# A two-layer hybrid network on one core: 512 columns per matmul in the dense products, activation buffers 64 bytes beyond a multiple of 128, norm totals from a rounded part and its rest

## What is computed

```python
def rmsnorm(x, g):
    y = x32 * lax.rsqrt(jnp.mean(x32 * x32, axis=-1, keepdims=True) + NORM_EPS)
    return (y * g).astype(x.dtype)
def conformer_conv(h, ...):            # layer 1 in place of the recurrence
    u = h @ w_in + b_in                # "cin"
    u = u[..., :D] * jax.nn.sigmoid(u[..., D:])
    u = causal_dwconv(u, dw) + dw_b    # 31 taps
    u = jax.nn.silu(layernorm(u, ln_g, ln_b))
    return u @ w_out + b_out           # "cout"
def conv_ffn(h, w_in, dw, w_out):      # "up" 1024 -> 5632, "down" 2816 -> 1024
    u = causal_dwconv(h @ w_in, dw)
    gate, val = u[..., :D_FF], u[..., D_FF:]
    return (jax.nn.silu(gate) * val) @ w_out
x = x + out; x = x + attention(rmsnorm(x, ..)); x = x + conv_ffn(rmsnorm(x, ..), ..)
```

## Time and profile before

| | |
|---|---|
| median of 3 runs | 2604.6 us (2602.82 to 2608.18) |
| profiled execution, on the device | 2604.33 us |
| its span, first to last instruction | 2602.5 us |
| instructions | 62231 |
| TensorE busy | 2506.9 us, 96% of the span, 25266 matmuls |
| VectorE, ScalarE, GpSimd busy | 1340.9, 1122.6, 995.2 us |
| mean granted TensorE clock | 0.986 |
| moved over DMA | 219.43 MB, mean 84 GB/s |

### The profile page before, as it was taken

One profiled execution on the slowest core, in us unless ns is written; L12 is line 12 of the kernel. 1 busy time (PEld: TensorE's weight loads), 2 busy tenths in 40 slices (PEclk: granted clock), 3 DMA queues, 4 the chain that ended last, 5 costly groups with the idle time before them and its releaser, 6 DMA issues.

```text
span 2602.5 us, 62231 instructions
## 1 busy us (share of the span) xinstructions
PE 2506.9 (96%) x25266; PEld 2367.6 (91%) x25266; DVE 1340.9 (52%) x2035; ACT 1122.6 (43%) x1652; POOL 995.2 (38%) x488
## 2 busy tenths in 40 slices
PE   6999898999999999998999999999999999999998
PEld 6888796997999999977989999999998769999998
DVE  7657554613477741798533677612143344455521
ACT  7834455454444433334534344433244444444422
POOL 3324220461444444325322444444443104444442
PEclk8899999999999999999999999999999999999999
DMA  4221001251232233323212322233222103322232
GB/s 147 74 65 59 2 1 63 82 194 38 94 97 95 91 102 100 130 65 105 90 65 65 97 94 91 92 111 114 88 93 69 49 1 97 97 89 97 96 99 74
DMA packets 62180, 219.43 MB, mean 84 GB/s; under 512 B 6752, under 2 KB 9184, under 8 KB 61408
## 3 DMA queue, kind: packets, MB, share of 16 engines
q1 hardware_dynamic: 58880, 207.76, 24.4%
q10 hardware_dynamic: 3168, 9.75, 1.1%
HBM read 213.29 MB, written 4.19 MB: 84 GB/s over the span
## 4 chain that ended last, share of the span: by engine, by line
PE 83%; DVE 8%; issue 6%; ACT 2%; POOL 1%; DMA 0%; DVEq 0%; POOLq 0%; ACTq 0%
PE psum L571 70%; DVE psum L2698 5%; PE psum L713 3%; PE psum L721 2%; PE psum L1072 1%; PE psum L1021 1%; PE psum L1251 1%; POOL wl L520 1%; PE psum L1290 1%; DVE psum L2267 1%; PE psum L1253 0%; ACT wh L1382 0%; PE psum L683 0%; PE psum L1278 0%; PE psum L690 0%
## 5 line engine op out<-in xcount | busy, mean ns | idle before, releaser
L520 POOL TENSOR_TENSOR wl<-raw,wh 128x1024 fp32r<-128x1024 f32 x388 | 949.0, 2455 | 1464.0 <-ACT wh L1382 1463.6
L571 PE MATMUL psum<-acth,wh 128*128 128x256 f32 x3792 | 763.8, 283 | 20.6 <-DVE actl L2789 8.2
L571 PE MATMUL psum<-actl,wh 128*128 128x256 f32 x3792 | 753.9, 281 | 0.0
L571 PE MATMUL psum<-acth,wl 128*128 128x256 f32 x3792 | 753.3, 280 | 0.0
L1382 ACT ACTIVATE wh<-raw 128x1024 fp32r<-128x1024 f32 x388 | 407.1, 1056 | 625.1 <-PE psum L571 601.4
L571 PEld LDWEIGHTS psum<-acth,wh 128*128 128x128 f32 x3792 | 582.7, 189 | 38.1 <-issue 30.2
L571 PEld LDWEIGHTS psum<-acth,wl 128*128 128x128 f32 x3792 | 581.7, 189 | 0.0
L571 PEld LDWEIGHTS psum<-actl,wh 128*128 128x128 f32 x3792 | 581.5, 189 | 0.0
L2628 DVE TENSOR_TENSOR cu<-psum,rstd 128x512 f32<-128x512 f32 x132 | 91.1, 690 | 236.9 <-PE psum L571 219.6
L571 PE MATMUL psum<-hidh,wh 128*128 128x256 f32 x1056 | 210.0, 277 | 0.0
L571 PE MATMUL psum<-hidh,wl 128*128 128x256 f32 x1056 | 209.5, 277 | 0.0
(11 more groups left out here) (442 smaller groups left out, 4048.3 us busy)
## 6 DMA issues: line engine op xcount, KB each, us to landing
raw<-in_weights SPq DMA_DIRECT2D x388, 512.0 KB, 3.3
xt<-in_x SPq DMA_DIRECT2D x4, 512.0 KB, 5.4
xt<-in_x ACTq DMA_DIRECT2D x1, 2048.0 KB, 9.3
out_x<-xt SPq DMA_DIRECT2D x6, 256.0 KB, 2.3
mem<-in_mem ACTq DMA_DIRECT2D x1, 1024.0 KB, 11.0
memn<-memh ACTq DMA_DIRECT2D x1, 1024.0 KB, 7.0
memn<-meml ACTq DMA_DIRECT2D x1, 1024.0 KB, 10.0
memh<-memn ACTq DMA_DIRECT2D x1, 1024.0 KB, 4.7
```

The source lines that it names most:

```text
L520: pool.tensor_tensor(wl[:, s, :], raw[:, s, :], wh[:, s, :].bitcast(F32), ALU.subtract).then_inc(split_done, 1)
L571: ins = pe.matmul(out[:, n:n + HALF], w, m[:, n:n + HALF], start=first and n == 0, stop=last and n + HALF >= out.shape[1])
```

## The change

- `product` issues one matmul for all columns of a term: 512, or 256 over the memory tokens.
- The cursor is moved on by 32 bytes ahead of `acth`, which lies at 67648 then, `actl` at 84032; small buffers change places behind them so that `zone` stays where it was. The ones become a buffer of their own of type fp32r, set by VectorE; `eps` shares a buffer with the parameters.
- The norm totals in front of xattn, ffn, conv, in2 and for the memory: ScalarE rounds the sum of squares into `sums[0]` (`sum_high`), VectorE subtracts for the rest `sums[1]` (`sum_low`), and TensorE sums both over the partitions in fp32r, four matmuls of 256 columns. The first norm, the layer norm and the last norm keep the fp32 total (`exact_total`).
- These totals come behind tile 1, where they came behind tile 0 (in o behind tile 2).

```diff
...
         n = KT if split else 0
-        self.take(stage, sq=KT, rstd=1, split=n, val=n)
+        self.take(stage, sq=KT, rstd=1, split=n, val=n, sums=n // KT)
...
         xt = place("xt", [P, KT, T + 1])
+        cursor[0] += 32
         act_at = cursor[0]
+        assert act_at % P == 64
         acth = place("acth", [P, KT, T], F32R)
         actl = place("actl", [P, KT, T], F32R)
-        par = place("par", [P, NPAR])
-        common = place("common", [P, 3 * P])
+        par = place("par", [P, NPAR + 6])
+        eps = par[:, NPAR:NPAR + 6]
+        sq_at = cursor[0]
+        sq = place("sq", [P, 2, T])
+        sums = at("sums", [P, 2, T], F32R, sq_at)
         omu = place("omu", [P, 7 * KT])
-        eps = place("eps", [P, 6])
+        common = place("common", [P, 2 * P])
+        ones_r = place("ones", [P, P], F32R)
         tmp_at = cursor[0]
         tmp = place("tmp", [P, 2, T])
-        sq_at = cursor[0]
-        sq = place("sq", [P, 2, T])
         rstd_at = cursor[0]
...
         zone = cursor[0]
-        ident, ones, blk64 = (common[:, j * P:(j + 1) * P] for j in range(3))
+        ident, blk64 = (common[:, j * P:(j + 1) * P] for j in range(2))
+        ones = ones_r[:, :].bitcast(F32)
+        assert zone % 512 == 192 and sq_at % 64 == 32
         b_eps, b_ln, b_gn, b_rn, b_q, b_eps2 = (eps[:, j:j + 1] for j in range(6))
...
-        room = [[act_at, act_at + 32768], [yx_at, yx_at + 16384], [xt_at, xt_at + 16384], [tmp_at, tmp_at + 10240]]
+        room = [[act_at, act_at + 32768], [yx_at, yx_at + 16384], [xt_at, xt_at + 16384], [tmp_at, tmp_at + 6144], [sq_at, sq_at + 4096]]
...
             sp.dma_start(common[:, :], dram["c_common"]).then_inc(common_in, 16)
-            sp.dma_start(par[:, :], dram["par"]).then_inc(par_in, 16)
+            sp.dma_start(par[:, 0:NPAR], dram["par"]).then_inc(par_in, 16)
             with sp.Fori(0, UNITS // SLOTS) as i:
...
                 for w, m, first, last in ((w_h, hi, start, False), (w_h, lo, False, False), (w_l, hi, False, stop)):
-                    for n in range(0, out.shape[1], HALF):
-                        ins = pe.matmul(out[:, n:n + HALF], w, m[:, n:n + HALF], start=first and n == 0,
-                                        stop=last and n + HALF >= out.shape[1])
+                    ins = pe.matmul(out, w, m, start=first, stop=last)
                 return ins
...
-            def norm_total(stage, n=T):
+            def exact_total(stage):
                 pe.wait_ge(sq_used, plan(stage, "sq") + KT + SC)
-                pe.matmul(bank[4][:, 0:n], ones, rstd[:, 0:n], start=True, stop=True).then_inc(sum_mm, 1)
+                pe.matmul(bank[4][:, :], ones, rstd[:, :], start=True, stop=True).then_inc(sum_mm, 1)
+
+            def norm_total(stage, n=T, to=4):
+
+                pe.wait_ge(sum_lo, plan(stage, "sums") + 1)
+                for j in range(2):
+                    for c in range(0, n, HALF):
+                        ins = pe.matmul(bank[to][:, c:c + HALF], ones_r[:, :], sums[:, j, c:c + HALF], start=j == 0 and c == 0,
+                                        stop=j == 1 and c + HALF >= n)
+                ins.then_inc(sum_mm, 1)
...
             pe.wait_ge(common_in, 16)
-            norm_total("norm0")
+            pe.wait_ge(ones_ready, 1)
+            exact_total("norm0")
             for b in (1, 2):
-                pe.matmul(bank[b][:, 0:3 * P], ones, common[:, :], start=True, stop=True)
-                pe.matmul(bank[b][:, 3 * P:T], ones, ident, start=True, stop=True)
+                for c in range(0, T, HALF):
+                    pe.matmul(bank[b][:, c:c + HALF], ones, common[:, :], start=c == 0, stop=c > 0)
...
                 tile("o", j, "post", acth, actl)
-                if j == 1:
+                if j == 2:
                     norm_total("norm_mem0", MEM)
...
                     tile("q1", 0, "norm_x1", headh, headl)
+                    tile("q1", 1, "norm_x1", headh, headl)
                     pe.wait_ge(vt_ready, 8)
                     norm_total("norm_x1")
-                    dense("q1", "norm_x1", headh, headl, units=4, skip=1)
+                    for j in range(2, 5):
+                        tile("q1", j, "norm_x1", headh, headl)
                     pe.wait_ge(evacuated, plan("q1", "tile") + 2 + UC)
...
                 tile(up, 0, norm, acth, actl)
+                tile(up, 1, norm, acth, actl)
                 norm_total(norm)
-                dense(up, norm, acth, actl, units=2 * FT - 4, skip=1)
-                for j in range(2 * FT - 3, 2 * FT):
+                dense(up, norm, acth, actl, units=2 * FT - 4, skip=2)
+                for j in range(2 * FT - 2, 2 * FT):
                     tile(up, j, norm, acth, actl)
...
                 tile("cin", 0, "norm_conv", acth, actl)
+                tile("cin", 1, "norm_conv", acth, actl)
                 norm_total("norm_conv")
-                dense("cin", "norm_conv", acth, actl, units=4, skip=1)
-                for j in range(5, 8):
+                dense("cin", "norm_conv", acth, actl, units=4, skip=2)
+                for j in range(6, 8):
                     tile("cin", j, "norm_conv", acth, actl)
...
                     tile("kv1b", j, "norm_mem0", memh, meml, n=MEM)
-                norm_total("ln")
+                exact_total("ln")
                 dense("cout", "ln", acth, actl)
...
                 tile("in2", 0, "norm_h", acth, actl)
+                tile("in2", 1, "norm_h", acth, actl)
                 pe.wait_ge(acc_ready, 1)
                 pe.matmul(bank[4][:, :], ones, acc_x[:, :], start=True, stop=True)
-                pe.matmul(bank[5][:, :], ones, acc_y[:, :], start=True, stop=True).then_inc(sum_mm, 1)
+                norm_total("norm_h", to=5)
...
-                inner(1, 12)
+                inner(2, 8)
+                for j in range(10, 13):
+                    tile("in2", j, "norm_h", acth, actl)
                 pe.wait_ge(evacuated, t0 + 13 + UC)
...
+            def sum_high(stage, n=T):
+
+                act.wait_ge(sq_used, plan(stage, "sq") + KT + SC)
+                act.activation(sums[:, 0, 0:n], rstd[:, 0:n], ACT.Identity).then_inc(sum_hi, 1)
+
             def x_is_ready(stage):
...
                         weight_high(UNIT0[stage] + (s + 1) * per - 1 + SLOTS, i, 4 * per)
+                if not gain:
+                    sum_high(norm)
...
+                act.wait_ge(acc_ready, 1)
+                act.activation(sums[:, 0, :], acc_y[:, :], ACT.Identity).then_inc(sum_hi, 1)
                 act.wait_ge(x_ready, plan("down1", "x") + KT + SC)
...
+            def sum_low(stage, n=T, of=rstd):
+
+                dve.wait_ge(sum_hi, plan(stage, "sums") + 1)
+                dve.tensor_tensor(sums[:, 1, 0:n], of[:, 0:n], sums[:, 0, 0:n].bitcast(F32), sub).then_inc(sum_lo, 1)
+
             def residual(stage, skip=0, count=KT):
...
                             dve.tensor_tensor(b[:, :], b[:, :], sq[:, (n * s + j) % 2, :], add).then_inc(sq_used, 1)
+                if n == 1:
+                    sum_low(norm)
...
+            dve.memset(ones_r[:, :].bitcast(F32), 1.0).then_inc(ones_ready, 1)
             dve.memset(xt[:, :, 0:1], 0.0)
...
                                              op0=mul, op1=add).then_inc(acc_ready, 1)
+                    sum_low("norm_h", of=acc_y)
                 else:
```

More of the change, by code:

```diff
@@ L90, in constants @@
     f = lambda m: m.astype(np.float32)
-    common = np.concatenate([f(s == t), np.ones((P, P), np.float32), f(same64)], 1)
+    common = np.concatenate([f(s == t), f(same64)], 1)
     tt = np.arange(64)[None, :]
@@ L120, in constants @@
     }
-CONST_COLS = {"c_common": 3 * P, "c_prep": 4 * 8, "c_core": 7 * CH, "c_post": 5 * P,
+CONST_COLS = {"c_common": 2 * P, "c_prep": 4 * 8, "c_core": 7 * CH, "c_post": 5 * P,
               "c_hybrid": T + 2 * P + 8 * P}
@@ L208, in build_program @@
         plan.take(f"down{l}", tile=8, x=KT)
-    plan.take("norm_h", sq=2 * KT, rstd=1, split=KT, val=KT, total=1)
+    plan.take("norm_h", sq=2 * KT, rstd=1, split=KT, val=KT, total=1, sums=1)
     plan.take("final", x=KT)
@@ L430, in build_program @@
         sum_mm, acc_ready = sem("sum_mm"), sem("acc_ready")
+        ones_ready, sum_hi, sum_lo = sem("ones_ready"), sem("sum_hi"), sem("sum_lo")
         dve_chain, act_chain = sem("dve_chain"), sem("act_chain")
@@ L1749, in _ @@
                 squares("norm_mem0", k, mem[:, k, :])
+            sum_high("norm_mem0", MEM)
             added_o(0)
@@ L1761, in _ @@
                 squares("norm_x0", k, x(k))
+            sum_high("norm_x0")
             def evac(stage, to, func=ACT.Identity, n=T, count=None, skip=0, bias=None):
@@ L2528, in _ @@
                 squares_added("norm_mem0", k, MEM)
+            sum_low("norm_mem0", MEM)
             for j in range(2):
@@ L2540, in _ @@
                 squares_added("norm_x0", k)
+            sum_low("norm_x0")
             def attention(l):
```

## The result

The changed kernel takes 2616.4 us (median of 6 runs, 2615.2 to 2622.2) against 2605.9 us of the kernel before in the same job: ratio 1.0037, 95% interval 1.0021 to 1.0053. It is slower by some 10 us, clear of the noise but small. The forecast was 2574, faster, with a range up to 2608.

What follows compares the result with a forecast made beforehand. The prediction took the pace of TensorE's matmuls as the bound (busy 96% of the span, 83% of the chain). Its terms: 2604.3 - 30 - 2.8 + 2.7 = 2574 us, range 2505 to 2608.

Steps and rivals of the forecast that it cites:

- The small moves: Ones set by memset, smaller constants' DMA, scratch buffers (the recurrence's too) at new addresses: 0, within 2 us either way.
- Part 1: acth and actl start 64 instead of 32 bytes beyond a multiple of 128: 116.7 to 113.3 ns, 30 us less.
- Part 2: Dense products as one matmul of 512 columns instead of two of 256: 226.7 ns, no gain of its own, 0.
- rival A: In dense products the loss comes once per matmul, so 512 columns cost 220 ns: 90 us together, 2514 us; chance 0.27.
- Rival B: In dense products 512 columns run at the slow pace, 233 to 235.6 ns: slower, 2614 to 2631 us; chance 0.14.
- Part 3: Seven norm totals over 512 columns leave fp32 for four matmuls of 256 columns, 0.45 us each: 2.8 us less.
- The weight margin in up: In up0, with the total behind the second tile, unit 4's weights are still ready 3 us early: no cost.
- VectorE sets the end until 1217 and can't make it good: In cin the later total delays the second evacuation from 1060.9 to 1063.6 us, lost for good: +2.7 us.
- the memory norm, 256 columns, stands in a stretch that waits for weights: 0: At the memory norm, the new total changes nothing because the stretch waits for weights anyway: 0.
- The prediction's marks: Signs against it: down under 118 or over 124 us, up still 5.6 us a unit, TensorE idle at up's fifth tile, head below 226 ns.

Runs made afterwards that it cites:

- e5: The changed kernel with each product again two matmuls of 256 columns, activations and new norm totals kept: 2635.1 us, ratio 1.0112.
- e2: The changed kernel with 160 idle instructions more at TensorE's start, so the recurrence's loop starts at 239 modulo 256 as before: 2602.4 us.
- e3: The kernel before with 96 idle instructions more at TensorE's start, so the recurrence's loop starts at 79 modulo 256 as in the changed kernel: 2637.9 us.
- e8: The changed kernel with 94 products of the last v tiles split into two matmuls, so the loop starts at 11 modulo 256: 2591.2 us.
- e12: The kernel before with only acth's start moved on by 32 bytes, two matmuls of 256 columns and fp32 totals kept: 2628.0 us, ratio 1.0083.
- e1: A separate kernel of fp32r products alone, operand start offsets varied, one matmul of 512 columns or two of 256: 226.7 to 240.1 ns a product.
- e7: The changed kernel with streamed buffers at multiples of 256 bytes and 80 products split, loop at 239 modulo 256: 2566.7 us, ratio 0.9848.
- e6: The kernel before with acth moved and one matmul per product, old fp32 totals kept behind tile 0: 2612.2 us, ratio 1.0023.

## Why the prediction was wrong

**The missing term, +23.5 us.** Under "The small moves" I priced what the change does to the recurrence at 0, within 2 us, and looked at its scratch addresses only (that their fp32 matmuls have "no loss of the kind above" was an estimate from the 0.86 us of a pair; e5, with these addresses moved, has steady rounds of 19.8 us, as before has). The change also takes 1440 instructions out ahead of its loop. No rival named that. e2 takes the loss back, e3 puts it into the kernel before. Without it after would be 12.6 us faster than before in the profiled executions, and e8, which is after with the loop at a good place, took 2591.2 us in its one run. That is half of the 30 us forecast or less, so the other terms were off as well.

**Part 1, -30 us forecast, +22.6 measured (e12).** The step that failed is "I price this as 116.7 to 113.3 ns". I had seen that 64 "allows 113.3 but doesn't guarantee it", with head as the exception, and then took the better value for 189 units. At this address 256 columns have two paces. Before, `acth` at 32 mod 64 has a mixed pattern of its own (the starts are 113 to 121 ns apart; e1 has the same 233.3 a product at 32), and down0, which follows, runs at 113.3; with `acth` at 64, the 117.8 that q0 and head showed persists through up and down alike. The bounds, 0 to 39 us of gain, left out a loss.

**Part 2, 0 forecast.** It left a product at twice 113.3 ns, 226.7. What speaks for it are the two matmuls of the earlier trace rows, together 0.34 us at 256 columns and 0.57 at 512, 115 ns for each further 256 columns. Whether a loss comes along with the columns, or once per matmul as rival A has it, no run shows, since none gives a pace without one; they show the pace of whole products, 226.7 ns at best with one matmul of 512 columns (e7), not rival A's 220 or 215. But "So 512 columns cost 226.7" needed the start at a multiple of 256: 228.8 for `acth` (4.6 ns gained where 6.7 were forecast), 233.3 for the zone's buffers (6.6 lost on hid where nothing was). Applied to the products of the prediction: acth 4536 x -4.6 = -21 us, hid 1584 x +6.6 = +10.5, y 192 x 6.6 = +1.3, head 576 x -2.3 = -1.3, q0 and out2 384 x -6.7 = -2.6: -13 us, and the trace has -12.6 outside the recurrence. Up and down bear this out by themselves (-14.6 for a measured -15.2, +10.5 for +10.6). That the total agrees is in part luck: the start and the output stages gained 10.3 us where the sum has 0.9 for v, and kv0 lost 5.2 where it has nothing. Against that, the one matmul of 512 columns rids the kernel of the two paces: e6 is 16 us faster than e12 with a slow recurrence.

**Rival B** had hid right (233 to 235.6 forecast, 233.3 measured) and its 2614 to 2631 us hold the result, but by another sum: it let acth gain at most 0.4 ns a product where it gained 4.6, and had no slow recurrence.

**Part 3.** The total takes 4 matmuls 0.12 us apart, 0.47 us (0.45 forecast). The weight margin in up held: no wait of TensorE from 698 to 730 us. In cin the second evacuation came 15.0 us after the stage's start (1063.86 to 1078.86; 14.9 forecast, 12.3 before), but the later start was made good: from cin to the second memory stage it is 125.5 us where it was 126.1. So "VectorE sets the end until 1217 and can't make it good" was wrong. And "the memory norm, 256 columns, stands in a stretch that waits for weights: 0" overlooked the total of x0 in the same stretch, where the weights' own chain waits for the new rounding: +3.0 us (e6).

**What would show it wrong.** The prediction's marks were down shorter than 118 us or longer than 124, up unchanged at 5.6 us a unit, and head below 226 ns. Down came to 123.2, between its two marks, a unit of up to 5.49 us, between the forecast 5.44 and 5.6, and head to 233.3 ns; none of the marks was reached, and none stood for the recurrence. The paces told the cases apart.

## What to carry to other kernels

When a change alters how many instructions stand ahead of a long hardware loop (1718 here; no other length was tried), look at the instruction queue and at the "issue" waits inside the loop first; the same code can be 1.4 times slower by its place, and some split products ahead of it put it right (94 in e8). For fp32r products stream 512 columns from buffers at a multiple of 256 bytes (226.7 ns; two matmuls of 256 columns cost 240 there); before pricing an alignment, measure the very pair of address and length in a small kernel, in two orders, since one reading can be one of two states. An instruction put in front of a queue's regular work is priced by what stands behind it, weights above all.

## What the hardware showed that I had not expected

- A loop of 1718 TensorE instructions runs its steady rounds without loading any, or loads 18 to 26 blocks in 98 us, by its place in the stream: 169.8 to 240.6 us for the same recurrence. In after the stalls of 4.1 and 3.8 us at the jump are each followed by a lower granted clock (0.61 over the 8 us from 300, 0.57 over the 8 us from 356).
- One matmul of 512 columns of fp32r: 226.8, 228.9 or 233.3 ns by its start modulo 256 (0, 64, other). Two of 256 columns: 226.7 or 235.5 at 64 and 192, 233.3 at 32, 237 to 240 at 128, 240 at 0 and 96.
- The pace of two matmuls of 256 columns at such an address is handed on from stage to stage: down0 lost 4.7 us (e12) with its own buffers, weights and instructions unmoved, when the operand of the stage ahead of it had moved. How it is handed on isn't shown.
